# V pages requested by ScalarE instead of SyncE, and weight panels one piece later in a two-layer decoder step

## The reference

```python
past_k = cache_sb_k[j][page_table].reshape(db, n_pages * cache_sb_k.shape[2], SB_HEADS, SB_HEAD_DIM)
past_v = cache_sb_v[j][page_table].reshape(db, n_pages * cache_sb_v.shape[2], SB_HEADS, SB_HEAD_DIM)
tok, mq, k, v = sb_mixer(h @ w_in_sb[j], sb_bias[j], past_k, past_v)
...
z = jnp.einsum('bqhd,bkhd->bhqk', q, kb) * scale + bias_f
log_fail = jnp.where(mask, jax.nn.log_sigmoid(-z), 0.0)
after = lax.cumsum(log_fail, axis=3, reverse=True) - log_fail
w = jnp.where(mask, jnp.exp(jax.nn.log_sigmoid(z) + after), 0.0)
outs.append(jnp.einsum('bhqk,bkhd->bqhd', w.astype(v.dtype), vb))
```

## Time and profile before

| what | value |
|---|---|
| median of 3 runs | 1911.52 us (1901.49 to 1913.43) |
| the profiled execution | 1920.76 us, of which 1919.1 us from the first to the last instruction |
| mean granted TensorE clock | 0.901 of full speed |
| TensorE busy | 1642.3 us, 86% of the span |
| VectorE, ScalarE, GpSimd busy | 744.6, 620.7, 557.0 us |
| moved by DMA | 325.96 MB, mean 170 GB/s |

### The profile page before, as it was taken

One profiled execution on the slowest core, in us unless ns is written; L12 is line 12 of the kernel. 1 busy time (PEld: TensorE's weight loads), 2 busy tenths in 40 slices (PEclk: granted clock), 3 DMA queues, 4 the chain that ended last, 5 costly groups with the idle time before them and its releaser, 6 DMA issues.

```text
span 1919.1 us, 25299 instructions
## 1 busy us (share of the span) xinstructions
PE 1642.3 (86%) x9377; PEld 1257.4 (66%) x9377; DVE 744.6 (39%) x1038; ACT 620.7 (32%) x1056; POOL 557.0 (29%) x522
## 2 busy tenths in 40 slices
PE   6589998875979799888889848998768899999997
PEld 4467665543657566666656536664337899999997
DVE  2650003134477565656647564013321322122121
ACT  3312225122244322342224232244322433243342
POOL 1221222000224223333323224321102344444443
PEclk9887999567989999999989879988878999999999
DMA  7664997732456787969886858620011232333322
GB/s 234 189 210 128 287 305 238 225 110 95 157 171 192 251 264 256 312 207 305 252 257 215 283 190 282 204 104 0 1 44 44 66 89 89 89 95 98 95 78 82
DMA packets 288482, 325.96 MB, mean 170 GB/s; under 512 B 13690, under 2 KB 205808, under 8 KB 288036
## 3 DMA queue, kind: packets, MB, share of 16 engines
q1 hardware_dynamic: 286168, 316.56, 51.8%
q0 software_dynamic: 2192, 7.78, 1.0%
HBM read 315.48 MB, written 8.99 MB: 169 GB/s over the span
## 4 chain that ended last, share of the span: by engine, by line
PE 63%; DVE 13%; DMA 6%; SPq 6%; ACT 5%; issue 4%; POOL 1%; DVEq 0%; ACTq 0%; POOLq 0%
PE PS L455 41%; PE PS L469 4%; SPq L1133 3%; DMA vring<-cache_sb_v 3%; PE PS L414 2%; DVE prod L2116 2%; PE PS L494 2%; SPq L1129 2%; PE PS L404 2%; PE PS L764 2%; DVE scr L2121 2%; PE PS L907 1%; PE PS L1005 1%; DMA kring<-w_ffn_up 1%; DVE scr L1843 1%
## 5 line engine op out<-in xcount | busy, mean ns | idle before, releaser
L1260 POOL TENSOR_TENSOR parts<-wring,parts 128x512 fp32r<-128x512 f32 (+1 forms) x400 | 518.1, 1296 | 1209.3 <-ACT parts L1349 1208.5
L455 PE MATMUL PS<-hh_r,parts 128*128 128x260 f32 (+1 forms) x2880 | 719.4, 339 | 13.4 <-DVE hl_r L1849 11.8
L455 PEld LDWEIGHTS PS<-hh_r,parts 128*128 128x128 f32 x2880 | 496.9, 192 | 105.6 <-issue 48.4
L1349 ACT ACTIVATE parts<-wring 128x512 fp32r<-128x512 f32 (+1 forms) x400 | 248.7, 623 | 897.4 <-PE PS L455 800.1
L455 PE MATMUL PS<-hl_r,parts 128*128 128x260 f32 (+1 forms) x1440 | 464.0, 335 | 0.0
L455 PEld LDWEIGHTS PS<-hl_r,parts 128*128 128x128 f32 x1440 | 276.7, 192 | 27.8 <-issue 1.7
L455 PE MATMUL PS<-E_r,parts 128*128 128x260 f32 (+1 forms) x1584 | 268.1, 329 | 3.4 <-issue 2.4
L455 PEld LDWEIGHTS PS<-E_r,parts 128*128 128x128 f32 x1584 | 232.2, 193 | 44.4 <-issue 19.9
L2116 DVE TENSOR_TENSOR prod<-kring,PS 128x1024 f32<-128x1024 f32 x128 | 150.1, 1213 | 19.3 <-DMA kring<-cache_sb_k 19.1
L2121 DVE TENSOR_REDUCE scr<-prod 128x16 f32<-128x1024 f32 x128 | 149.7, 1212 | 0.0
L2296 DVE TENSOR_TENSOR xT<-xT,PS 128x512 f32<-128x512 f32 (+1 forms) x64 | 44.2, 691 | 239.1 <-PE PS L455 239.1
(11 more groups left out here) (278 smaller groups left out, 1554.8 us busy)
## 6 DMA issues: line engine op xcount, KB each, us to landing
vring<-cache_sb_v SPq DMA_DIRECT2D x256, 256.0 KB, 3.8
kring<-cache_sb_k SPq DMA_DIRECT2D x256, 256.0 KB, 3.7
wring<-w_ffn_up SPq DMA_DIRECT2D x88, 512.0 KB, 5.4
wring<-w_ffn_down SPq DMA_DIRECT2D x16, 1024.0 KB, 5.0
kring<-w_ffn_up SPq DMA_DIRECT2D x12, 1024.0 KB, 10.7
vring<-w_ffn_up SPq DMA_DIRECT2D x10, 1024.0 KB, 11.0
wring<-w_mem_kv SPq DMA_DIRECT2D x8, 1024.0 KB, 6.6
wring<-w_in_gla SPq DMA_DIRECT2D x8, 1024.0 KB, 5.9
```

The costliest lines, as they stand in the source:

```text
L455: last = mm(PS[:, bank + c, 0:w], parts[:, q, a, P * k:P * k + P], x[:, k0 + kk, o:o + w], start=(q == 0 and k == 0 and a == 0 and x is sr ...
L1260: gp.tensor_tensor(part_as(n, 1, src, w), src, part_as(n, 0, src, w), ALU.subtract).then_inc(wlo_ok, 1)
L1349: return fn(dst, src, ACT.Copy)
```

## The change

The function that requests four pages becomes common to the engines and takes the engine as an argument. K pages are still requested by SyncE. V pages are requested by ScalarE: groups 0 and 1 ahead of the out projection of layer 0, and group 8 b + g + 2 in paged step 9 b + g + 14, one step after the one in which TensorE uses the group that was in the slot. In the blocks below, "ISA" rows are register operations.

In SyncE's program the weight panels are also placed one piece later: panel g goes to the position of piece 2 (g - 2) + 1 instead of 2 (g - 2).

```diff
+        def pages(eng, cache, ring, arrived, n):
+            b, g = n // KGROUPS, n % KGROUPS
+            o = b * PAGES + PAGES - 4 - 4 * g
+            _, numbers = nc.values_load_multi_w_load_instructions(
+                pt[0:1, o:o + 4], engines=[eng.engine], min_val=0, max_val=I[cache].shape[1] - 1)
+            for jj in range(4):
+                page = numbers[3 - jj]
+                eng.dma_start(ring[:, n % 2, jj, :],
+                              I[cache][0, bass.ds(page, 1)].rearrange("a p h d -> (a p) (h d)")).then_inc(arrived[n % 2], 16)
...
             def k_pages(n):
                 if n < 2:
                     sp.wait_ge(s_free[n], 18)
                 else:
                     sp.wait_ge(k_used, n - 1)
-                pages("cache_sb_k", kring, k_in, n)
-
-            def v_pages(n):
-                if n < 2:
-                    sp.wait_ge(s_free[2 + n], 17)
-                else:
-                    sp.wait_ge(v_used, n - 1)
-                pages("cache_sb_v", vring, v_in, n)
+                pages(sp, "cache_sb_k", kring, k_in, n)
...
             for pos in range(S_POS + 100):
-                while g < 2 * PANELS and piece_position(2 * (g - 2)) <= pos:
+                while g < 2 * PANELS and piece_position(2 * (g - 2) + 1) <= pos:
                     panel(g)
                     g += 1
...
-                while vn < 64 and (sample_position(S_PANEL_STEP[66 + vn]) if vn < 2 else
-                                   kv_position(9 * ((vn - 2) // 8) + 13 + (vn - 2) % 8)) <= pos:
-                    v_pages(vn)
-                    vn += 1
...
+            def v_pages(n):
+                if n < 2:
+                    act.wait_ge(s_free[2 + n], 17)
+                else:
+                    act.wait_ge(v_used, n - 1)
+                pages(act, "cache_sb_v", vring, v_in, n)
+
             def paged():
                 for t in range(KV_STEPS):
...
+                    b, g = (t - 14) // 9, (t - 14) % 9
+                    n = KGROUPS * b + g + 2
+                    if t >= 14 and g < KGROUPS and n < KGROUPS * NB:
+                        v_pages(n)
                     yield
...
             q_column(0)
+            act.wait_ge(pt_in, 16)
+            v_pages(0)
+            v_pages(1)
             out_projection(0, PROMPT)
```

More of the change, by code:

```diff
@@ L1122, in sample_panel @@
                 sp.dma_start(dst, src).then_inc(s_in[s], 16)
[L1124 to L1134, removed]
             def k_pages(n):
@@ L1170, in _ @@
             sp.dma_start(pt[:, :], I["page_table"].rearrange("(a b) n -> a (b n)", a=1)).then_inc(pt_in, 16)
-            g, r, kn, vn = 2, 4, 0, 0
+            g, r, kn = 2, 4, 0
             for pos in range(S_POS + 100):
-                while g < 2 * PANELS and piece_position(2 * (g - 2)) <= pos:
+                while g < 2 * PANELS and piece_position(2 * (g - 2) + 1) <= pos:
                     panel(g)
@@ L1209, in _ @@
                     kn += 1
-                while vn < 64 and (sample_position(S_PANEL_STEP[66 + vn]) if vn < 2 else
-                                   kv_position(9 * ((vn - 2) // 8) + 13 + (vn - 2) % 8)) <= pos:
-                    v_pages(vn)
-                    vn += 1
-            assert (r, kn, vn) == (S_PANELS, 64, 64), (r, kn, vn)
+            assert (r, kn) == (S_PANELS, 64), (r, kn)
             while g < 2 * PANELS:
```

## The result

The changed kernel takes 1956.72 us (median of 4 runs, 1952.49 to 1959.47) against 1912.24 for the kernel before (4 runs, 1901.49 to 1913.43). The ratio is 1.0239, 95% interval 1.0209 to 1.0269: **slower by 44.5 us**. The forecast was 1914, its range ended at 1952. The profiled execution has a span of 1954.9 us against 1919.1, so the traces show 35.8 us of the 44.5; the rest is that the execution profiled before was 0.5% above its median.

What follows compares the result with a forecast made beforehand. TensorE was taken to wait 58.1 us for V pages standing behind K requests that wait for VectorE. Terms -58 + 38 + 8 + 2 + 19 - 3 - 3 = +3 us on the 1911.5 us median: 1914 us, range 1876 to 1952.

Steps and rivals of the forecast that it cites:

- V waits, old out and new in: TensorE's 58 us of waits for V pages go; 38 us of new ones come with requests on ScalarE.
- held splits: On ScalarE, weight splits start late behind V page requests: 8 us lost, bounds 0 and 15.
- late panels: Weight panels 19, 52 and 54 arrive late for TensorE: 19 us lost, bounds 8 and 40.
- K pages: On SyncE, K pages no longer wait for a V request: 3 us back for TensorE, bounds 0 and 8.
- groups 0 and 1: Their V requests on ScalarE delay a split before the paged steps: 2 us lost, bounds 0 and 4.
- the first stage: Sample panels go out ahead of their piece's weight panel, so TensorE waits less: 3 us back, bounds 0 and 7.
- Part 2: V pages requested by ScalarE arrive 8.0 us after the request starts, leaving 38 us of V waits, bounds 13 and 73.
- The walk: Step through V groups 2 to 63, shifting each request and use: 30 us of waits at 7.7 us latency.
- shared transfer engines: Rival: both queues share transfer engines, a group takes 9.0 us to its use, V waits 68: 1950 us, chance 0.12.
- Part 4: On SyncE, weight panels stand behind K requests waiting for VectorE; panels 19, 52 and 54 late, 19 us lost.
- Part 3: On ScalarE, V requests delay work behind them: 8 us for weight splits, 2 us for the first two groups.
- Part 5: SyncE's shorter queue gives back 3 us in the first stage and 3 us through earlier K pages.

Runs made afterwards that it cites:

- e4: The changed kernel with only the first stage's weight panels (2 to 13) one piece later, all other panels at their old positions; 1926.68 us.
- e7: e4 with each K page transfer from group 2 on bringing only the first 128 of 512 columns; 1918.1 us.
- e3: The kernel before with only the first stage's weight panels (2 to 13) one piece later, V pages still on SyncE; 1903.5 us.
- e8: e3 with ScalarE waiting for v_used and loading page numbers twice where the change requests V pages, without a DMA; 1905.2 us.
- e10: The kernel before with V pages ahead of the K pages of their position in SyncE's program, nothing else changed; 1842.09 us.
- e6: e3 with V pages ahead of the K pages of their position in SyncE's program; 1835.69 us.

## Why the prediction was wrong, point by point

The prediction's sum for the profiled execution was +3 us, and 35.8 were measured there. By the first table:

| term | predicted | measured |
|---|---|---|
| V waits, old out and new in | -58 + 38 = -20 | +3.7 (61.8 for 58.1) |
| held splits, late panels, K pages, groups 0 and 1 | 8 + 19 + 2 - 3 = +26 | +27.9 (other idle, 16.5 and 11.4) |
| the same TensorE work takes longer, by the clock | not in the sum | +13.2 (4.8 and 8.4) |
| the first stage | -3 | -9.2 |
| behind the pages | 0 | +0.2 |

**The step that failed is Part 2, the latency.** The mechanism was right: one piece of 6.85 us is shorter than the time from request to use, and ScalarE's queue runs ahead of its arithmetic. The walk was right too, as its own table of latencies shows: it gave 49 us of V waits at 8.4 us and 68 at 9.0. What failed is the 8.0 us that I put into it, 7.7 from one group and a mean of eleven landings and 0.3 for the overlap. From the first load to the last landing it was 8.8 us on average over the 62 groups, for which I read some 61 us between these two entries, and 61.8 were measured. It was 8.0 before the change already, so 0.3 of the 0.8 us was missing from the start, and the overlap cost 0.8 and not 0.3. In the 24 groups of clear waits it was 9.4 us, 3.5 from the load to the last request's end and 5.9 behind it, where the earlier trace rows had 3.05 and 4.56. I had counted the overlap with K pages only. In the trace after, 53 of the 62 groups have a panel's transfer under way as well, and the last page lands 5.7 us after the last request in these and 3.6 in the other nine. The panels' move is not the reason: in e4, where they stand in their old places, it is also 53 groups, with 66.0 us of V waits. The rule that the prediction cited against the change (the Trainium skill, DMA: Bandwidth & Descriptors, Issuing engines are not separate DMA queues) described this overlap; the traces agree, with a median V landing of 4.9 us beside full K pages (e4) and 3.8 beside quarter ones (e7), where one queue had 3.8 before. The rival built on it, shared transfer engines at 1950 us, came nearest, and 0.12 was too little for it.

**No term for the last stage.** I checked V latency against the long stretch, where V waits exist, and let each group's gain and loss cancel. In the in-projection of layer 1 there was nothing to gain (3.0 us of V waits) and a full step to lose (13.7). The walk of 62 groups contained these groups, but its 7.7 us was too short to make them wait.

**A clock term was missing.** 13.2 us of the loss is the same instructions running longer. TensorE was busy at the lower clock for 71.6 us of the long stretch (64.0 before) and 31.8 of the last (13.3 before), and half of the difference is 13.0 us. In the windows around and after the 10 us gap the granted clock is 0.77 to 0.91, where before it was 1.00.

**Part 4, panels behind K requests: right in kind, roughly right in size.** Panel 19's gap was 6.4 us (predicted 7.5) and panel 54's 10.0 (7.7); panel 52's grew only from 0.8 to 1.3 (by 3.6 predicted). But ScalarE waited for w_ffn_up in ten places, not one, since `k_used` waits grew from 161.4 to 419.0 us. Against e4, other idle time is 13.4 and 9.9 us more, 23 for the 19, of which 3.3 stand at TensorE's wait for VectorE ahead of the memory panels. That the sum came out near 19 is partly luck: panel 52 was hardly late, and gaps of up to 2.4 us at panels that I had called in time made up for it.

**Part 3, held splits: the direction right, the price uncertain.** e4 against e3 has 3.0 us more of other idle time in the long stretch, or 7.3 without its last gap, for my 8, while a hold without requests cost nothing measurable (e8).

**Part 5, the first stage: undersized.** 9 us in the traces and 8.5 in the timed e3, for 3. I priced only TensorE's waits for sample panels. Idle time there fell by 4.3 us and the rest by 4.9, of which the clock explains 1.5 by the same estimate (busy at the lower level for 145.6 us, 148.7 before); but kernels with the same first stage differ by up to 10 us there (488.3 to 498.5), so this split is loose.

**What I missed altogether.** The prediction said that V pages are late because they stand behind a K request that waits for VectorE. That was nearly the whole diagnosis, and e10 acts on it with one swap on the same queue for 67 us; 9.7 of the 58 us of V waits are left in its trace. The change took V off that queue and gave the gain away with the step.

## What to carry to other kernels

When a request is late because it stands behind another's wait, first reorder the queue: put the request whose wait ends earlier ahead. If it moves to another engine, count its lead from the slot's release to the next use, and compare it with the latency of requests that coincide with the other queue's transfers, all of them, and not with one taken from a single queue. And ask in each stage whether the request was late there at all: a step of lead given away costs most where it had been on time.

## What the runs showed of the hardware

Idle time of TensorE costs more than itself. Between the out projection and layer 1, e6 has 43.5 us less V idle time than before and 5.2 less of other, but is 69.0 us shorter (550.4 against 619.4): the same 2304 instructions take 20.4 us less beside it, 507.6 for 527.9. TensorE is busy at the lower clock for 21.0 us of it instead of 64.0, and half of that difference is 21.5. The windows over the two stretches, of before and of e6, have a granted clock of 0.92 and 0.97:

```profile
502.00:1121.00 619.00, 528.13 (x2306) 373.52 (x2304) 384.99 (x437) 206.81 (x330) 193.31 (x155) 0.92 0.76 245
```

```profile
491.00:1042.00 551.00, 508.18 (x2308) 360.94 (x2307) 387.35 (x438) 206.56 (x330) 193.63 (x155) 0.97 0.84 275
```

So a us of idle time that came back was worth about 1.4 us here. It also worked the other way: in the last stage e4 has 12.5 us more idle time than e3 and is 20.9 us longer.
